# Expert weights moved, waited for and given back in halves of a ring slot

## The reference

```python
eid = g_idx * EXPERTS_PER_GROUP + e_idx
...
def expert(args):
    xb, e = args
    return (jax.nn.silu(xb @ w_g[e]) * (xb @ w_u[e])) @ w_d[e]
...
out = out.at[row_tok].add(y * row_w[:, None])
```

```python
hp = _rmsnorm(x, norm_ple_g[i])
x = x + (p[i] @ w_ple[i]) * jax.nn.sigmoid(hp @ w_ple_gate[i])
```

## Time and profile before

| | |
|---|---|
| median of 3 runs | 707.93 us |
| the runs | 706.35 to 708.38 us |
| the profiled execution, its own time | 705.55 us |
| its span, first to last instruction | 703.8 us |
| TensorE busy in the span | 645.2 us (92%) |
| moved by the 16 DMA engines | 174.75 MB, mean 248 GB/s |
| mean granted TensorE clock | 0.985 |

### The profile page before, as it was taken

One profiled execution on the slowest core, in us unless ns is written; L12 is line 12 of the kernel. 1 busy time (PEld: TensorE's weight loads), 2 busy tenths in 40 slices (PEclk: granted clock), 3 DMA queues, 4 the chain that ended last, 5 costly groups with the idle time before them and its releaser, 6 DMA issues.

```text
span 703.8 us, 11016 instructions
## 1 busy us (share of the span) xinstructions
PE 645.2 (92%) x4332; PEld 485.4 (69%) x4335; DVE 365.0 (52%) x640; ACT 282.1 (40%) x445; POOL 73.9 (10%) x82
## 2 busy tenths in 40 slices
PE   4999999899999999999999999799999977688694
PEld 3899997599999999995797888544444432234273
DVE  5686964868677666675786574621222110112245
ACT  5773472656555555545847621201101100010275
POOL 1000000400000000003085500000000000000181
PEclk9999999999999999999999999999999999999999
DMA  9763541747755555106704159999599999999901
GB/s 325 253 218 121 183 146 61 258 143 251 233 191 190 192 187 179 60 0 224 271 7 161 73 214 426 423 409 426 235 430 425 428 428 427 427 424 430 385 7 60
DMA packets 54345, 174.75 MB, mean 248 GB/s; under 512 B 4647, under 2 KB 29347, under 8 KB 47907
## 3 DMA queue, kind: packets, MB, share of 16 engines
q1 hardware_dynamic: 53632, 172.54, 63.9%
q10 hardware_dynamic: 674, 1.69, 0.6%
HBM read 173.17 MB, written 1.05 MB: 248 GB/s over the span
## 4 chain that ended last, share of the span: by engine, by line
PE 71%; DMA 13%; DVE 8%; ACT 5%; issue 2%; ACTq 0%; DVEq 0%
PE ps L1725 14%; PE ps L1727 14%; PE ps L1726 14%; DMA arena<-in_w_moe_dram 13%; PE ps L2224 6%; PE ps L2234 4%; PE ps L2210 3%; PE ps L2259 3%; PE ps L1914 2%; PE ps L2062 1%; DVE arena L1409 1%; ACT wpg_high L975 1%; DMA hh<-in_conv_ffn_dram 1%; PE ps L1743 1%; PE ps L2013 1%
## 5 line engine op out<-in xcount | busy, mean ns | idle before, releaser
L1725 PE MATMUL ps<-hT_high,w_up_high 128*128 128x256 f32 x352 | 99.7, 283 | 0.0
L1727 PE MATMUL ps<-hT_high,w_up_low 128*128 128x256 f32 x352 | 99.6, 283 | 0.0
L1726 PE MATMUL ps<-hT_low,w_up_high 128*128 128x256 f32 x352 | 99.6, 283 | 0.0
L1725 PEld LDWEIGHTS ps<-hT_high,w_up_high 128*128 128x128 f32 x352 | 67.5, 192 | 0.9 <-DVE w_up_low L1245 0.5
L1726 PEld LDWEIGHTS ps<-hT_low,w_up_high 128*128 128x128 f32 x352 | 67.5, 192 | 0.3
L1727 PEld LDWEIGHTS ps<-hT_high,w_up_low 128*128 128x128 f32 x352 | 67.5, 192 | 0.0
L1245 DVE TENSOR_TENSOR w_up_low<-W,w_up_high 128x1024 fp32r<-128x1024 f32 x44 | 53.3, 1239 | 23.9 <-ACT w_up_high L790 23.9
L790 ACT CAST w_up_high<-W 128x1024 fp32r<-128x1024 f32 x44 | 44.6, 1047 | 28.6 <-PE ps L1727 28.6
L949 ACT ACTIVATE arena<-ps 128x256 f32<-128x256 f32 x9 | 3.4, 383 | 117.3 <-PE ps L2224 117.3
L1725 PE MATMUL ps<-h_high,dense_high 128*128 128x256 f32 x160 | 45.8, 286 | 0.0
L1726 PE MATMUL ps<-h_low,dense_high 128*128 128x256 f32 x160 | 45.3, 283 | 0.0
(11 more groups left out here) (465 smaller groups left out, 1385.1 us busy)
## 6 DMA issues: line engine op xcount, KB each, us to landing
W<-in_w_moe_dram SPq DMA_DIRECT2D x25, 2048.0 KB, 19.8
arena<-in_w_moe_dram SPq DMA_DIRECT2D x19, 2048.0 KB, 25.4
W<-in_w_up_dram SPq DMA_DIRECT2D x22, 1024.0 KB, 8.3
W<-in_w_in_dram SPq DMA_DIRECT2D x8, 2048.0 KB, 10.9
W<-in_w_down_dram SPq DMA_DIRECT2D x11, 1024.0 KB, 5.0
hh<-in_w_moe_dram SPq DMA_DIRECT2D x4, 2048.0 KB, 28.7
W<-in_w_out_dram SPq DMA_DIRECT2D x2, 2048.0 KB, 9.0
W<-in_w_o_dram SPq DMA_DIRECT2D x2, 2048.0 KB, 7.9
```

Source lines behind the costliest of these rows:

```text
L1725: pe.matmul(o, lhs[0], rhs[0], start=first, stop=False, skip_group_check=True)
L1726: pe.matmul(o, lhs[0], rhs[1], start=False, stop=False, skip_group_check=True)
L1727: return pe.matmul(o, lhs[1], rhs[0], start=False, stop=last_k, skip_group_check=True)
```

## The change

Each ring item is transferred as two halves, by two transfers that both add to the slot's semaphore, which is therefore waited for at 32 a use instead of 16. In memory and in the slot an up chunk is laid out by inner step first, then expert, then column, so that its first half holds the first inner step of all 4 experts. A down chunk is laid out by column half first, the half that is multiplied first in front. A half is 1 MB, 8 KB in each partition. TensorE signals after each inner step of an up chunk and after each column half of a down chunk, so `upw_used` rises by 8 a round (`UPH`) and `downw_used` by 4 (`DNH`). SP waits for each half of the old item and then issues the same half of the new one. TensorE still waits for the whole of a chunk before it reads it. The host's layout follows.

```diff
--- before.py
+++ after.py
@@ -52,6 +52,7 @@
 NGRP8 = N_EXP // COLS
 MAXR = SEQ // CAP
 UPC, DNC = 4, 2
+UPH, DNH = 2 * UPC, 2 * DNC
 CPG = UPC + DNC
 NCHUNK = NGRP8 * CPG
 UNIT = 4096
@@ -354,11 +355,11 @@
 
         def up_chunk(n):
 
-            return ring(item(n)).rearrange("p (c k n) -> p c k n", c=COLS, k=2)
+            return ring(item(n)).rearrange("p (k c n) -> p c k n", c=COLS, k=2)
 
         def down_chunk(n):
 
-            return ring(item(n)).rearrange("p (c n) -> p c n", c=COLS)
+            return ring(item(n)).rearrange("p (s c n) -> p c s n", s=2, c=COLS)
 
         def par_c(name, i, n=1):
             c = col[name] + i
@@ -396,6 +397,7 @@
         ukv = W[:, 2 * UNIT + 2048:2 * UNIT + 3072]
         wm = W[:, 3 * UNIT:3 * UNIT + 1536].rearrange("p (m h e) -> p m h e", m=3, h=M_HEADS)
         w_moe = a["w_moe"]
+        w_ple = a["w_ple_2"][0].rearrange("(k p) n -> p k n", p=P)
         wple = ring(PLE_AT)[:, 0:2048].rearrange("p (k n) -> p k n", k=2)
         wpg = [ring(NCHUNK + 1 + h).rearrange("p (k n) -> p k n", k=KD) for h in range(2)]
         assert (NCHUNK + 1) % RING == 5 and (NCHUNK + 2) % RING == 6
@@ -502,32 +504,38 @@
             sp.dma_start(PAN[4], w_o[:, :, 0:512]).then_inc(sig("wo0_landed"), 16)
 
 
-            def load_chunk(n):
-                g, j = divmod(chunk_of(n), CPG)
-                sp.dma_start(ring(n), w_moe[g, j]).then_inc(sig(f"ring{n % RING}_landed"), 16)
+            def load_half(n, part):
+
+                landed = sig(f"ring{n % RING}_landed")
+                if n == PLE_AT:
+                    sp.dma_start(wple[:, part:part + 1, :], w_ple[:, part:part + 1, :]).then_inc(landed, 16)
+                elif n <= NCHUNK:
+                    g, j = divmod(chunk_of(n), CPG)
+                    o = slice(part * UNIT // 2, (part + 1) * UNIT // 2)
+                    sp.dma_start(ring(n)[:, o], w_moe[g, j][:, o]).then_inc(landed, 16)
+                else:
+                    h = n - NCHUNK - 1
+                    o = slice(4 * part, 4 * part + 4)
+                    sp.dma_start(wpg[h][:, o, :], w_pg[:, o, 512 * h:512 * h + 512]).then_inc(landed, 16)
 
             for n, (name, count) in enumerate((("uq_used", 1), ("st_done", 6), ("pv_done", 4), ("y1_high", 5), ("num_done", 4),
                                                ("half_used", 1), ("ym_ready", at("ym_ready", 2)), ("wo_used", 1), ("wo_used", 1),
                                                ("wo_used", 1), ("logits_done", at("logits_done", 2)))):
                 sp.wait_ge(sig(name), count)
-                load_chunk(n)
+                for part in range(2):
+                    load_half(n, part)
 
             sp.wait_ge(sig("rounds_ready"), 1)
             for n in range(RING, NITEM):
                 g, j = divmod(n - RING, CPG)
                 if j == 0:
                     ends = sp.value_load(rint[0:1, 8 + g:9 + g], min_val=1, max_val=NGRP8 * MAXR)
-                if j < UPC:
-                    sp.wait_ge(sig("upw_used"), ends * UPC + (j + 1))
-                else:
-                    sp.wait_ge(sig("downw_used"), ends * DNC + (j - UPC + 1))
-                if n == PLE_AT:
-                    sp.dma_start(wple, a["w_ple_2"][0].rearrange("(k p) n -> p k n", p=P)).then_inc(sig(f"ring{n % RING}_landed"), 16)
-                elif n <= NCHUNK:
-                    load_chunk(n)
-                else:
-                    h = n - NCHUNK - 1
-                    sp.dma_start(wpg[h], w_pg[:, :, 512 * h:512 * h + 512]).then_inc(sig(f"ring{n % RING}_landed"), 16)
+                for part in range(2):
+                    if j < UPC:
+                        sp.wait_ge(sig("upw_used"), ends * UPH + (2 * j + part + 1))
+                    else:
+                        sp.wait_ge(sig("downw_used"), ends * DNH + (2 * (j - UPC) + part + 1))
+                    load_half(n, part)
             assert NITEM - 1 - RING < PLE_AT
             sp.wait_ge(sig("out_ready"), 1)
             sp.dma_start(out[0, 0:P, :], hn[:, 0, :]).then_inc(sig("stored"), 16)
@@ -945,13 +953,13 @@
 
             def act_step(n):
 
-                act.wait_ge(sig("upw_used"), n * UPC + 2 * UPC)
+                act.wait_ge(sig("upw_used"), n * UPH + 2 * UPH)
                 act.activation(sg, ps[:, 2, 0:F_EXP], ACT.Silu).then_inc(sig("sg_ready"), 1)
                 act.wait_ge(sig("oht_done"), n + 2)
                 act.copy(SC, ps[:, 0, 0:256]).then_inc(sig("sc_ready"), 1)
                 act.wait_ge(sig("at_done"), n + 2)
                 act.copy(aT, v3(ps[:, 3, 0:256], 2)).then_inc(sig("aT_ready"), 1)
-                act.wait_ge(sig("downw_used"), n * DNC + 2 * DNC)
+                act.wait_ge(sig("downw_used"), n * DNH + 2 * DNH)
                 act.copy(Yp[:, 1, :], ps[:, 2, :]).then_inc(sig("ypb_ready"), 1)
                 act.copy(Yp[:, 0, :], ps[:, 3, :]).then_inc(sig("ypa_ready"), 1)
 
@@ -971,7 +979,7 @@
                 for n in pieces:
                     h, q = divmod(n, 4)
                     m = NCHUNK + 1 + h
-                    act.wait_ge(sig(f"ring{m % RING}_landed"), 16 * (m // RING + 1))
+                    act.wait_ge(sig(f"ring{m % RING}_landed"), 32 * (m // RING + 1))
                     act.copy(wpg_high[h][:, 2 * q:2 * q + 2, :], wpg[h][:, 2 * q:2 * q + 2, :]).then_inc(sig("dense_high"), 1)
 
             def round_hp(js):
@@ -2193,11 +2201,11 @@
             keep_busy(2, 3)
             pe.wait_ge(sig("rounds_ready"), 1)
             pe.wait_ge(sig("step_clear"), 2)
-            for name, n in (("gxa_done", 1), ("gxb_done", 1), ("oht_done", 1), ("at_done", 1), ("upw_used", UPC), ("downw_used", DNC)):
+            for name, n in (("gxa_done", 1), ("gxb_done", 1), ("oht_done", 1), ("at_done", 1), ("upw_used", UPH), ("downw_used", DNH)):
                 pe.sem_inc(sig(name), n)
 
             def landed_chunk(n):
-                pe.wait_ge(sig(f"ring{n % RING}_landed"), 16 * (n // RING + 1))
+                pe.wait_ge(sig(f"ring{n % RING}_landed"), 32 * (n // RING + 1))
 
             def gather(n, g):
 
@@ -2223,7 +2231,7 @@
                         for c in range(COLS):
                             last = pe.matmul(ps[CAP * c:CAP * c + CAP, 2, :], xg[:, k, CAP * c:CAP * c + CAP],
                                              up_chunk(CPG * g + j)[:, c, kk, :], start=(k == 0), stop=(k == KD - 1))
-                    last.then_inc(sig("upw_used"), 1)
+                        last.then_inc(sig("upw_used"), 1)
 
             def scatter(n, signal="scatter_done"):
 
@@ -2257,9 +2265,9 @@
                     for half, bank in ((1, 2), (0, 3)):
                         for c in range(COLS):
                             last = pe.matmul(ps[CAP * c:CAP * c + CAP, bank, :], aT[:, f, CAP * c:CAP * c + CAP],
-                                             down_chunk(CPG * g + UPC + f)[:, c, 512 * half:512 * half + 512],
+                                             down_chunk(CPG * g + UPC + f)[:, c, 1 - half, :],
                                              start=(f == 0), stop=(f == 1))
-                    last.then_inc(sig("downw_used"), 1)
+                        last.then_inc(sig("downw_used"), 1)
 
             def pe_step(n, g):
                 gather(n, g)
@@ -2334,8 +2342,9 @@
 
     laid_out["rows"] = _np.concatenate([_np.asarray(inputs[name]).reshape(-1, P) for name, _ in ROWS])
     up = _np.concatenate([_np.asarray(inputs[name])[0] for name in ("w_gate_e_2", "w_up_e_2")], axis=2)
-    up = up.reshape(NGRP8, COLS, UPC, 2, P, 2 * F_EXP).transpose(0, 2, 4, 1, 3, 5).reshape(NGRP8, UPC, P, UNIT)
-    down = _np.asarray(inputs["w_down_e_2"])[0].reshape(NGRP8, COLS, DNC, P, D).transpose(0, 2, 3, 1, 4).reshape(NGRP8, DNC, P, UNIT)
+    up = up.reshape(NGRP8, COLS, UPC, 2, P, 2 * F_EXP).transpose(0, 2, 4, 3, 1, 5).reshape(NGRP8, UPC, P, UNIT)
+    down = _np.asarray(inputs["w_down_e_2"])[0].reshape(NGRP8, COLS, DNC, P, 2, D // 2)
+    down = down[:, :, :, :, ::-1].transpose(0, 2, 3, 4, 1, 5).reshape(NGRP8, DNC, P, UNIT)
     laid_out["w_moe"] = _np.concatenate([up, down], axis=1)
     lr = _np.asarray(inputs["w_in"])[0][:, C_LR:C_LR + 32].reshape(KD, P, 32).transpose(1, 0, 2)
     laid_out["w_lr"] = _np.concatenate([lr[:, :, 0:16], lr[:, :, 0:16], lr[:, :, 16:32]], axis=2)
```

## The result

The changed kernel takes 708.83 us, median of 20 runs (705.18 to 710.63), and the kernel before in the same sessions 707.22 us (20 runs). The ratio is 1.0026, 95% interval 1.0015 to 1.0038: slower by 1.6 us on the medians, 1.1 to 2.7 us by the interval. The prediction had 709.6 us, +1.7 us. It took 0.3% (2.1 us) for the limit of what can be told; with 20 runs of each kernel the interval lies wholly above 1, so this smaller loss can be told.

A forecast was written before the change was run, and what follows sets the result against it. Transfers, not TensorE, were taken to bound the second half of the expert stage. Restart -0.87 us plus packets +2.6 us gave +1.7 us on the median of 707.93 us: 709.6 us, range 706.7 to 712.

The forecast's parts named there:

- The restart: At the hole (DMA share 0.24 in 495:501 us), earlier release of a half restarts transfers earlier: -0.87 us.
- The packets: Behind the hole, 8 KB runs instead of 16 KB make each of 31 chunks 0.084 us dearer: +2.6 us.
- the doubled closing packets: Each transfer's very small last packet on each engine doubles in number: +9 ns a chunk.
- The rule on fixed costs: About 2 us per transfer, an estimated 62 us for 31 more; prediction rejected it for queued transfers.
- Costs put at nothing: SP's extra issues and waits, TensorE's extra signals, and the layout: 0 us; the queue stays far from dry.
- A: Rival, expert transfers: smaller packets cost nothing, rate stays 428 GB/s, only -0.87 us is left, 707.1 us; chance 0.18.
- B: Rival, expert transfers: halves cost 0.10 us a chunk or more, net +2.2 us upward, 714.5 at the bound; chance 0.17.
- C: Rival, group 7: TensorE becomes the bound through slow-clock spells; two more give 711.3 us; chance 0.07.
- D: Rival, the hole: it closes further than by half a chunk, a gain over 2.1 us; chance 0.06.

The follow-up runs named there:

- e1: The changed kernel, but SP waits for a whole item to be used before issuing either half: 709.23 us, ratio 1.0030.
- e5: The changed kernel's layout and signals, but only item 17, first behind the hole, moved and released in halves: 704.98 us, ratio 0.9978.
- e11: The changed kernel itself, unaltered, measured and profiled again: 709.04 us, ratio 1.0021.
- e2: The kernel before, each expert chunk still one transfer with one release, but stored in two blocks, so 8 KB runs: 709.64 us, ratio 1.0040.
- e8: The changed kernel plus 14 matmuls of zeros in TensorE's wait before the gate product: 707.86 us, ratio 1.0000.
- e10: The kernel before plus only the 14 matmuls of zeros before the gate product: 707.14 us, ratio 0.9993.
- e4: The kernel before, each expert chunk moved by two transfers of 64 partitions, still 16 KB runs, released whole: 708.07 us, ratio 1.0004.
- e3: The kernel before, each expert chunk still one transfer, but stored in four blocks, so 4 KB runs: 713.31 us, ratio 1.0083.

## Why the prediction was right

The mechanism came out as written, a small gain at the hole against a dearer packet behind it. That the sum of +1.7 us meets the medians' +1.6 us so closely is partly luck: the term of the packets was 0.4 to 0.7 us too large, and the medians show 0.3 to 0.5 us more than the stage does, for which no run has a sure cause. The chances leaned on three runs before, which spread over 0.29%, and gave "no change that can be told" 0.54.

*The restart, -0.87 us.* Measured 0.86 us in all profiles with an early release, and gone in e1. It was worth nothing behind the hole, as said: SP's issues there are still held up (six in 14.78 us from 566.42), and e5 keeps the gain with one slot.

*The packets, +2.6 us.* Right in kind and a little too large. B to L grew by 2.17 us in the change and 2.14 in e11, by 2.35 and 2.51 in e1 and e2, or by 1.95 us on the means of the change, e8 and e11 against before and e10. The pitch went up by 0.07 to 0.09 us a chunk for the 0.084 reckoned. The straight line through 16 KB and 2 KB gave 421 to 422 GB/s for 8 KB and the rows show 421. The price of the doubled closing packets, 0.3 us in the sum, is not measured: e4 has 0.39 or 0.13 us by the profile that it is set against, less than two profiles of before differ by. The few tenths between the change and e2 are of that size too.

*The rule on fixed costs.* "SBUF — State Buffer" in the Trainium skill, section "The DMA setup-cost knee", would have made e4 an estimated 62 us slower. The trace does not agree for queued transfers: e4's stretch B to L was 0.39 us longer. No run here shows what a transfer costs outside of a full queue, so this says nothing on that case. The other rule, 3 cycles a packet in "DMA: Bandwidth & Descriptors" in the Trainium skill, section "Why small descriptors are slow", comes to an estimated 0.9 us for e2 and 2.6 us for e3; the measured 2.3 to 2.5 and 6.8 to 7.1 us are over two and a half times that, so the rows were the better guide.

*Costs put at nothing.* The waits and issues of SP, the additional signals and the layout: e5 has the signals and the layout, and its stage is 0.6 us shorter than before's. The queue holds little more than half the time (26 to 30 us from issue to landing for 42 to 48, where the prediction reckoned 22 if the queue's room is counted in packets), and did not run dry. What its room counts is not settled: in 540:620 e4, with transfers of 1 MB like the change's, has medians of 37 to 40 us, and e2, with 2 MB in runs of 8 KB, 32 to 33 us. So it is neither bytes nor transfers alone.

*The rivals.* A (the packets cost nothing) falls with the pitch. B (0.10 us a chunk or more) falls too: 0.07 to 0.09 us. C (TensorE the bound in group 7): the last wait grew to 1.53 us, so the transfers stayed the bound. D (faster) is ruled out by the interval. The sum was +1.7 us; the stage gives -0.86 + 2.17 = +1.31 us in the first pair of profiles, -0.86 + 1.95 = +1.09 us on the means, and the medians +1.6 us.

## What to carry to other kernels

While the queue of transfers was full here, earlier release of its buffers bought nothing: look for the stretches where the DMA engines stand idle, and split only the transfer that ends such a hole, and the one that the end waits for. Splitting along the contiguous run of each partition makes shorter packets, and here these were paid for at every transfer; count packets before transfers. Here halving one slot and the last chunk beat both kernels, where halving everything lost to the one it started from.

## What was not expected of the hardware

The time of a packet was linear in its size: 428, 421, 408 and 387 GB/s for runs of 16, 8, 4 and 2 KB, which is a fixed part of 9 to 10 ns a packet on each engine. A second transfer per chunk with the same packets made B to L 0.39 us longer over 31 chunks, or 0.13 us, inside the 0.5 us by which two profiles of the same code differ.

The start of the expert stage moved between 453.73 and 459.10 us over these profiles, and for the very same kernel between 455.07 (the change) and 459.10 us (e11). That is several times the effect studied, and is why the stage had to be read from its own start.
